# A scan's exponents from running sums: another division of work among the engines, and separate loads for attention

## What is computed

```python
a = (dt * A).reshape(bsz, nc, CHUNK, g, r).transpose(0, 3, 4, 1, 2)
a_cum = jnp.cumsum(a, axis=-1)
lmat = jnp.exp(segsum(a))                  # exp(cum[l] - cum[s]) for s <= l
cb = jnp.einsum('bclgn,bcsgn->bgcls', cc, bc)
y_diag = jnp.einsum('bgcls,bgrcls,bcsgrp->bclgrp', cb, lmat, xc)
...
y_off = jnp.einsum('bclgn,bcgrpn,bgrcl->bclgrp', cc, prev_states, jnp.exp(a_cum))
y = (y_diag + y_off).reshape(bsz, length, g, r, p)
...
y = y_f + flip(y_b) + d_skip.astype(f32).reshape(g, r)[:, :, None] * xs
gated = y.reshape(...) * jax.nn.silu(zs)
gated = gated * lax.rsqrt(jnp.mean(gated * gated, axis=-1, keepdims=True) + EPS)
```

## Time and profile before

| what | us |
|---|---|
| median of three runs (3631.65 to 3635.02) | 3632.8 |
| the profiled execution | 3636.8 |
| its span | 3635.2 |
| busy PE / DVE / ACT / POOL | 2951.8 / 2194.0 / 1100.2 / 654.5 |
| decays, first load of the carry at | 831.3 |
| scan loop: first load, last store issued | 921.0, 1389.5 |
| attention: first fill, first score | 2197.8, 2232.9 |

### The profile page before, as it was taken

The page is one execution under the profiler, slowest core; times in us unless marked ns, Lnnn a source line. Parts: engine busy times, 40 slices in busy tenths (PEclk is TensorE's granted clock), DMA queues, the critical chain, the costliest instruction groups (busy, mean ns, idle before and its releaser), DMA issues.

```text
span 3635.2 us, 33851 instructions
## 1 busy us (share of the span) xinstructions
PE 2951.8 (81%) x12604; PEld 2154.2 (59%) x12604; DVE 2194.0 (60%) x2858; ACT 1100.2 (30%) x1415; POOL 654.5 (18%) x378
## 2 busy tenths in 40 slices
PE   7999869985576666996998993879598839999993
PEld 3777746642354443444777782768344438888882
DVE  6499935326666773333563695983122269999995
ACT  3122211000011110111323411657211127777772
POOL 2322000000433330000021002545210001111111
PEclk9999979986777877998999996999798969999996
DMA  5332266413111114112544217511522539999995
GB/s 191 110 108 99 80 207 218 151 67 127 67 64 52 58 38 178 73 59 65 139 119 116 68 72 130 84 29 35 197 70 102 193 124 402 412 415 412 414 412 213
DMA packets 250064, 560.85 MB, mean 154 GB/s; under 512 B 26729, under 2 KB 157401, under 8 KB 232614
## 3 DMA queue, kind: packets, MB, share of 16 engines
q1 hardware_dynamic: 176518, 423.64, 32.5%
q0 software_dynamic: 30032, 64.18, 6.5%
q10 hardware_dynamic: 43344, 70.79, 5.2%
HBM read 438.09 MB, written 120.45 MB: 154 GB/s over the span
## 4 chain that ended last, share of the span: by engine, by line


## 5 line engine op out<-in xcount | busy, mean ns | idle before, releaser
L2327 DVE TENSOR_TENSOR e_low<-e_raw,e_high 128x4096 fp32r<-128x4096 f32 x99 | 438.0, 4426 | 69.5 <-ACT e_high L2321 69.3
L2321 ACT ACTIVATE e_high<-e_raw 128x4096 fp32r<-128x4096 f32 x99 | 359.5, 3633 | 32.8 <-DVE live L2278 26.5
L128 PE MATMUL banks<-p_w_high,p_high 128*128 128x512 f32 (+1 forms) x640 | 250.2, 391 | 18.0 <-DVE p_w_low L1455 18.0
L128 PE MATMUL banks<-p_w_low,p_high 128*128 128x512 f32 (+1 forms) x640 | 246.1, 385 | 0.0
L128 PE MATMUL banks<-p_w_high,p_low 128*128 128x512 f32 (+1 forms) x640 | 245.8, 384 | 0.0
L965 PE MATMUL banks<-s_R,mats 128*128 128x384 f32 x256 | 131.9, 678 | 130.4 <-DVE s_R L953 82.6
L128 PE MATMUL banks<-c_w,c_mT 128*128 128x512 f32 x512 | 225.8, 597 | 9.4 <-DMA c_w<-in_w_out 9.4
L128 PE MATMUL banks<-e_high,e_xhigh 128*128 128x512 f32 x528 | 211.0, 400 | 9.1 <-issue 7.3
L483 DVE SCALAR_TENSOR_TENSOR acc<-img,taps,acc 128x1024 f32<-128x1024 f32 x160 | 209.8, 1311 | 5.7
L128 PE MATMUL banks<-h_high,w_high 128*128 128x512 f32 (+1 forms) x544 | 201.2, 370 | 9.2 <-POOL w_low L355 4.5
L128 PE MATMUL banks<-e_high,e_xlow 128*128 128x512 f32 x528 | 207.9, 394 | 0.0
(11 more groups left out here) (451 smaller groups left out, 6467.9 us busy)
## 6 DMA issues: line engine op xcount, KB each, us to landing
e_raw<-in_exp_w SPq DMA_DIRECT2D x99, 2048.0 KB, 10.7
mod_w<-in_ada_w SPq DMA_DIRECT2D x24, 1024.0 KB, 6.2
s_X<-xtok SPq DMA_DIRECT2D x19, 1024.0 KB, 4.9
p_raw<-in_w_in SPq DMA_DIRECT2D x18, 1024.0 KB, 5.9
y<-e_y ACTq DMA_DIRECT2D x33, 512.0 KB, 10.5
xbcT<-res ACTq DMA_DIRECT2D x20, 640.0 KB, 2.9
xtok<-xt ACTq DMA_DIRECT2D x20, 640.0 KB, 3.7
w_raw<-in_w_in SPq DMA_DIRECT2D x12, 1024.0 KB, 6.7
```

The costliest lines, as they stand in the source:

```text
L128: last = pe.matmul(out, a, b, start=start and n == 0, stop=stop and n == len(pairs) - 1)
L2321: act.activation(self.high[p % HIGHS][:], self.raw[p % RAWS][:], ACT.Copy).then_inc(*self.high_done.up())
L2327: dve.tensor_tensor(self.low[p % HIGHS][:], self.raw[p % RAWS][:], self.high[p % HIGHS][:].bitcast(F32), ALU.subtract).then_inc(*self.low_ ...
```

## The change

**Decays.** `a` becomes local to the stage. 16 more matmuls of 128 columns compute the running sums transposed, [24 heads, 128 tokens] for each chunk and way; ACT copies them to SBUF, SP stores them to a scratch tensor `cumT` (8, 2, 24·128) in DRAM. Two small tables are new: `gap`, forward minus backward running sum, and `back`, minus the backward one.

**The scan.** For each group SP loads the rows of `cumT` to all 128 partitions (two buffers, `load_sums`). `differences` on DVE takes for each head min(rowF - gap, rowB); `exponents` takes Exp with the bias `back` for each head, in place. This gives the forward decay at and above the diagonal, and the backward one below. Both `weights` and both `timed` run on DVE. The state parts come first in PE's order (`from_states`), ACT scales them out of PSUM per head (`scale`, 12 copies of 64 columns), and PE adds them to the chunk's product with the unit matrix (`both`). DVE's `gather` is one addition. The state steps group by group. The gate's squares are ACT's. POOL has only `skip_and_weigh`. z has one buffer. The order is one loop over n with the next group's weights and the second next group's differences.

**Attention.** The fills no longer read `far` but the constant zero, POOL's and SP's loads don't wait for all of them; the first pair's operands are loaded at once, except the two last rows of `fkl`, which wait for that buffer's fill; then `far` and `fv`, the second pair, tiles and keys, `dv` last. The first weighing waits for `fv` alone.

```diff
+        sums, sums_copied, sums_stored = s1.sb("s_sums", [NH, NT, 2, P]), s1.sem("s_sums_copied"), s1.dma("s_sums_stored")
...
+        for c in range(NT):
+            for w, m in enumerate((C_LE, C_GE)):
+                last = pe.matmul(core.bank[0:NH, 3 + c // 2, 256 * (c % 2) + P * w:256 * (c % 2) + P * w + P], a[:, c, NH * w:NH * w + NH],
+                                 tables["mats"][:, m, :], start=True, stop=True)
...
+        dve.tensor_tensor(t["gap"][:], p[:, 0:NT, 0:NH], p[:, 0:NT, NH:2 * NH], ALU.subtract).then_inc(*vec.up())
+        dve.tensor_scalar(t["back"][:], p[:, 0:NT, NH:2 * NH], -1.0, None, ALU.mult).then_inc(*vec.up())
+        act.wait_ge(*summed.at(2))
+        act.activation(sums[:].rearrange("p c w n -> p (c w n)"), core.bank[0:NH, 3:7, :].rearrange("p b n -> p (b n)"), ACT.Copy).then_inc(*sums_copied.up())
+        sp.wait_ge(*sums_copied.at(1))
+        sp.dma_start(dram["cumT"].rearrange("c w (h n) -> h c w n", n=P), sums[:]).then_inc(*sums_stored.up())
...
+        def load_sums(n):
+            c, g = n // NBC, n % NBC
+            if n >= 2:
+                sp.wait_ge(*diffed.at(n - 1))
+            sp.dma_start(sums[n % 2][:].rearrange("p w h n -> p w (h n)"),
+                         row(dram["cumT"][c, :, HG * P * g:HG * P * g + HG * P])).then_inc(*sums_in[n % 2].up())
...
+        def load_z(c):
+            if c:
+                sp.wait_ge(*z_used.at(c))
...
+            for h in range(HG):
+                last = dve.scalar_tensor_tensor(out=E[n % 2][:, h, :], in0=sums[n % 2][:, 0, h, :], scalar=col("gap", c, HG * g + h),
+                                                in1=sums[n % 2][:, 1, h, :], op0=ALU.subtract, op1=ALU.min)
...
+            for h in range(HG):
+                last = act.activation(E[n % 2][:, h, :], E[n % 2][:, h, :], ACT.Exp, bias=col("back", c, HG * g + h))
...
+        def scale(n):
+            act.wait_ge(*off_summed.at(n + 1))
             if n:
+                act.wait_ge(*summed.at(n))
             for w in range(2):
+                for h in range(HG):
+                    at = slice(HP * h, HP * h + HP)
+                    last = act.activation(y2[w][:, at], core.bank[:, y0 + 1 + w, at], ACT.Copy, scale=col("ec", c, NH * w + HG * g + h))
+            last.then_inc(*scaled.up())
...
+        def both(n):
+            pe.wait_ge(*scaled.at(n + 1))
+            for w in range(2):
+                last = pe.matmul(core.bank[:, 2 + 3 * (n % 2), 0:384], mats[:, C_ID, :], y2[w][:], start=False, stop=w == 1)
+            last.then_inc(*summed.up())
...
+        def roots(c):
+            act.wait_ge(*z_used.at(c + 1))
+            if c:
+                act.wait_ge(*gated.at(c))
             for g in range(NBC):
+                act.activation(sq[:], yts[c % 2][:, 384 * g:384 * g + 384], ACT.Square, accum_out=ss[:, g:g + 1]).then_inc(*squared.up())
+                act.wait_ge(*squared.now())
+            act.activation(sd[:], ss[:], ACT.Sqrt, bias=tables["eps"][:, 0:1], scale=1.0 / 384).then_inc(*rooted.up())
...
+        load_chunk(0), load_sums(0), load_sums(1)
+        sp.dma_start(skip[:], row(dram["d_skip"])).then_inc(*rows_in.up())
+        sp.dma_start(nw[:], row(dram["ssd_norm_w"])).then_inc(*rows_in.up())
+        load_chunk(1), load_z(0)
...
+        tensor_pairs(0), skip_and_weigh(0), skip_and_weigh(1)
+        differences(0), exponents(0), differences(1), exponents(1), timed(0, 0), timed(1, 0), vector_pairs(0), weights(0)
+        for n in range(N + 1):
+            c, g = n // NBC, n % NBC
+            if n:
+                gather(n - 1), vector_step(n - 1)
+            if n < N:
+                from_states(n), scale(n), within_chunk(n), tensor_step(n), both(n)
+            if n + 1 < N:
+                weights(n + 1)
+            if n + 2 < N:
+                load_sums(n + 2), differences(n + 2), exponents(n + 2)
+            if g == 0 and c:
+                gate(c - 1), roots(c - 1)
+            if g == 1 and c:
+                if c + 1 < NT:
+                    load_chunk(c + 1)
+                if c < NT:
+                    load_z(c)
+            if g == 1 and c + 1 < NT:
+                tensor_pairs(c + 1)
+            if g == 2 and c:
+                norm(c - 1), store(c - 1)
+                if c + 1 < NT:
+                    skip_and_weigh(c + 1)
+            if g >= 2 and c + 1 < NT:
+                timed(g - 2, c + 1)
+            if g == 2 and c + 1 < NT:
+                vector_pairs(c + 1)
+        norm(NT - 1), store(NT - 1)
...
-        load_fox(0), load_tile(0), load_tile(1)
+        load_fox(0)
+        sp.wait_ge(*far_emptied)
+        sp.dma_start(far[:, :, SEQ - P:SEQ], dram["far"].rearrange("m p n -> p m n")).then_inc(*masks_in.up())
+        sp.dma_start(fv[:], pv[:, :, C_FV:C_FV + 512]).then_inc(*values_in[0].up())
+        load_fox(1), load_tile(0), load_tile(1)
...
-        load_fox(1)
+        for half in range(2):
+            sp.dma_start(dv[:, :, half, :], pv[:, :, C_DV:C_DV + HD]).then_inc(*values_in[1].up())
```

More of the change, by code:

```diff
@@ L805, in decays @@
         dve.wait_ge(*vec.at(4))
-        dve.scalar_tensor_tensor(out=t["a"][:], in0=t["dt"][:], scalar=-1.0, in1=over(an[:], 1, n),
+        dve.scalar_tensor_tensor(out=a[:], in0=t["dt"][:], scalar=-1.0, in1=over(an[:], 1, n),
                                  op0=ALU.mult, op1=ALU.mult).then_inc(*vec.up())
@@ L895, in state_space @@
         cbs = [s.sb(f"s_cb{b}", [P, 2, NBC, P]) for b in range(2)]
+        sums = [s.sb(f"s_sums{b}", [P, 2, HG, P]) for b in range(2)]
         xfs = [[s.sb(f"s_xf{b}{w}", [P, DS]) for w in range(2)] for b in range(2)]
-        R = [s.sb(f"s_R{w}", [P, HG, P]) for w in range(2)]
         E = [s.sb(f"s_E{b}", [P, HG, P]) for b in range(2)]
@@ L921, in sync, with load_chunk @@
+        def load_chunk(c):
             b, at = c % 2, slice(P * c, P * c + P)
@@ new lines, in exponents, with weights @@
+        def exponents(n):
+            c, g = n // NBC, n % NBC
+            act.wait_ge(*diffed.at(n + 1))
+            for h in range(HG):
+                last = act.activation(E[n % 2][:, h, :], E[n % 2][:, h, :], ACT.Exp, bias=col("back", c, HG * g + h))
+            last.then_inc(*E_done.up())
+        def weights(n):
+            c, g = n // NBC, n % NBC
+            dve.wait_ge(*E_done.at(n + 1))
+            dve.wait_ge(*cb_done.at(c + 1))
+            if n >= 2:
+                dve.wait_ge(*summed.at(n - 1))
+            for w in range(2):
+                last = dve.tensor_tensor(M[n % 2][w][:], E[n % 2][:], over(cbs[c % 2][:, w, g, :], 1, HG), ALU.mult)
+            last.then_inc(*M_done.up())
@@ L969, in exponents @@
-        def exponents(c, g):
-            n = 4 * c + g
-            act.wait_ge(*diffed.at(n + 1))
-            if n >= 2:
-                for w in range(2):
-                    act.wait_ge(*M_done[w].at(n - 1))
-            act.activation(E[g % 2][:].rearrange("p (a h) n -> p a (h n)", a=2), core.bank[:, 0:2, 0:384], ACT.Exp).then_inc(*E_done.up())
-        def weights(e, w, c, g):
-            n = 4 * c + g
-            e.wait_ge(*E_done.at(n + 1))
-            e.wait_ge(*cb_done.at(c + 1))
-            if n >= 2:
-                e.wait_ge(*summed.at(n - 1))
-            e.tensor_tensor(M[g % 2][w][:], E[g % 2][:], over(cbs[c % 2][:, w, g, :], 1, HG), ALU.mult).then_inc(*M_done[w].up())
@@ L1015, in gather @@
+        def both(n):
+            pe.wait_ge(*scaled.at(n + 1))
+            for w in range(2):
+                last = pe.matmul(core.bank[:, 2 + 3 * (n % 2), 0:384], mats[:, C_ID, :], y2[w][:], start=False, stop=w == 1)
+            last.then_inc(*summed.up())
+        def gather(n):
+            c, g, y0 = n // NBC, n % NBC, 2 + 3 * (n % 2)
             y = yts[c % 2][:, 384 * g:384 * g + 384]
             dve.wait_ge(*summed.at(n + 1))
-            if n:
-                dve.wait_ge(*gathered.at(n))
@@ new lines, in tensor_step, with vector_step @@
+        def tensor_step(n):
+            c, g = n // NBC, n % NBC
+            pe.wait_ge(*weighed.at(c + 1))
+            if n:
+                pe.wait_ge(*stepped.at(n))
+            pe.matmul(core.bank[:, 1, 0:384], Xs[c % 2][:, DS + NST * g:DS + NST * g + NST], xds[c % 2][:, 384 * g:384 * g + 384],
+                      start=True, stop=True).then_inc(*stepping.up())
+        def vector_step(n):
+            c, g = n // NBC, n % NBC
+            state = H[:, 384 * g:384 * g + 384]
+            dve.wait_ge(*stepping.at(n + 1))
+            dve.tensor_tensor(heads(state), heads(state), over(col("et", c, HG * g, HG), 2, HP), ALU.mult).then_inc(*vec.up())
+            dve.wait_ge(*vec.now())
+            dve.tensor_tensor(state, state, core.bank[:, 1, 0:384], ALU.add).then_inc(*stepped.up())
@@ L1068, in vector_gate, with norm @@
+        def norm(c):
+            yt = yts[c % 2]
             dve.wait_ge(*rooted.at(c + 1))
@@ L1112, in scalar @@
-        def scalar(c):
-            if c == 0:
-                exponents(0, 0), exponents(0, 1)
```

(11 more changed lines are left out.)

245 lines of the change are left out of this document (92 added, 153 removed).

## The result

The changed kernel takes 3460.2 us (median of 4 runs, 3459.0 to 3461.1) against 3632.2 (3629.2 to 3635.0): a ratio of 0.9523, 95% interval 0.9512 to 0.9535, faster by 172 us. The forecast was 3503: the sign held and so did most of the mechanism, the gain was 43 us larger than forecast, and the time lies at the very edge of the range's low end. The profiled execution took 3461.1 us (its span 3459.4), 175.7 less than that of before, where the sum had 130.0.

What follows compares the result with a forecast made beforehand. The prediction took a ring of waits, with no engine full, to bound the scan. From 3636.8 us, scan -120.8, decays +8.8 and attention -18 gave 3506.8, less 4.0 for the runs' median: 3503, range 3460 to 3580.

Steps and rivals of the forecast that it cites:

- 31/4 x 38 = 294.5: Scan loop: the 31 groups after the first, four to a chunk, at 38 us per chunk against 53.4 before.
- ACT's chain: Scan, from g = 0: gate, squares, root, scaled copies, then PE's adding matmuls, done at 15.7 us warm or 17.4 cold.
- the 1.6 us for the cold matmuls: Scan chunk: 1.6 us more because the adding matmuls run cold behind PE's wait.
- the lock: Scan: DVE and POOL keep each other out; POOL's two instructions cost DVE 2.8 us per chunk, ends 0 and 5.5.
- +8.8 forecast: Decays stage: 16 new matmuls at the low clock, copy, issue and store add 8.8 us; 6 if the clock rises, or 11.
- First group, tail, attention: Scan's first group 43.0 us, its tail 10.2 us; attention 18 us shorter, ends 8 and 27.
- the wait behind the roots: Scan: after g = 1 DVE idles for ACT's chain, a new wait of 3.8 to 5.5 us per chunk.
- The ring of waits: Old scan loop: R on DVE and POOL, differences on PE, Exp on ACT, weights, and again; it sets the pace.
- B: Rival, scan: PE stays at 1.2 GHz, 50.4 us per chunk, 3599; partial case 3540 to 3580; chance 0.17 for both.
- C: Rival, scan: ACT's copies cheap, weigh and skip hidden, no cold spells; 31.5 us per chunk, 3453; chance 0.13.
- D: Rival, scan: the row loads make it slower; at 30 us per load 63.2 us per chunk, 3698; chance 0.05.
- E: Rival, attention: the edit does nothing, as the same bytes must land before the first score; 3521; chance 0.07.

Runs made afterwards that it cites:

- pool_small: Changed kernel with both of POOL's instructions per chunk cut to one head, leaving out the other 23: 3408.7 us, 32.5 us per chunk.
- timed_early: Changed kernel with both time weightings of the next chunk put at g = 2: 3467.2 us, ratio 0.9541, 35.2 us per chunk.
- att_only: Kernel before the change with the attention edit alone: 3619.7 us, ratio 0.9963.
- roots_late: Changed kernel with squares and root moved behind the next group's scaled copies on ACT: 3463.4 us, ratio 0.9530, 34.1 us per chunk.
- both orders: Changed kernel with the reorderings of roots_late and timed_early together: 3463.0 us, ratio 0.9528, 34.5 us per chunk.
- the same orders without POOL's work: Changed kernel with both orders and POOL's two instructions cut from 24 heads to one: 3395.2 us, 29.8 us per chunk.

## What the prediction had right, and which step failed

The profiled execution was forecast at 3506.8 and took 3461.1. The failed step is the term "31/4 x 38 = 294.5" for the groups behind the first: it measured 252.5 (first addition 967.60, last 1220.13), 42.0 of the 45.7 us. It failed twice.

- **The 38: 29 us over 7.75 chunks.** The chunk took 34.3 (33.5 to 35.4). From the opening addition to the third, the forecast had ACT's chain with cold adding matmuls, 6.8 + 5.1 + 3.8 + 1.6 = 17.3; measured 15.4 (mean of six). The chain was well priced: gate done after 6.6, squares and root 4.3, copies 2.4, sum 1.6, together 14.9 in the chunk shown (forecast 15.7 with PE warm). What failed is the 1.6 us for the cold matmuls. In five of the six chunks they took 1.45 to 1.56 us, at a clock of 1.00 in the chunk shown, where PE had stood only 0.38 us before them; in the first, behind a stop of 3.72 us, they took 2.93 at 0.50, and there this stretch took 16.3. The stop and the low clock lie at g = 0 instead, where the forecast had no wait, and inside the time that ACT's chain takes anyway. From the third addition to the next opening one, the forecast had 10.5 + 6.8 + 2.8 + 0.6 = 20.7, measured 18.9: DVE's own work 16.6 instead of 17.3, the lock 2.0 in the chunk shown instead of 2.8, and of the 0.6 for waits it couldn't place 0.24.
- **The 31/4: 13 us.** It gave the first three groups and the last four the average price of a group. At the measured 34.3 they would be 60.0 us; they took 20.1 and 26.8. The first three have no gate, norm, roots or late weightings, the last four no weightings, masks or POOL work. The list of a chunk's work stood in the same text; it only had to be crossed out for the two ends.

The other terms:

- **Decays: 4.4.** +8.8 forecast, +4.4 measured. 8.2 us for 16 matmuls were priced at the low clock, 0.51 each; they took 3.67, 0.23 each, at a granted clock of 1.00 (full tiles of 128 columns take 0.26 each at that clock: L959 at 1071.89, 8 records in 1.05). So this was the forecast's own other end, "6 if the clock rises", and not a matter of the narrower stationary tile. Copy (1.85) and store (2.8) were right. The carry behind them took 0.5 us less than before.
- **First group, tail, attention: -1.** 43.0 forecast, 42.7 measured from the first load at 924.91 to 967.60, and inside it POOL's four instructions did stretch the first differences (12 in 13.31 us; 6 take 1.66 alone). Tail 10.2 against 10.0. Attention 18 against 17.5 at the first score and 16.3 at the end.

What held: the price of a difference (6 in 1.66, spaced 0.26 as forecast), no wait for the sums (4.2 us to landing, forecast 5), the place of ACT's chain. ACT's load was 22.7 us in the chunk against 25.6: the copies last 0.34 us (forecast 0.35) but start 0.20 apart (forecast 0.26). Exp and copies together are 24 x 0.29 + 48 x 0.20 = 16.6 us by these spacings, which is the estimate of 16.5 that the prediction set beside its own 19.9. That the forecast of the third addition stood within 2 us owes something to luck: it had one chain there, the trace has two of the same length. DVE alone would be there after 11.6 us; PE's late sum (1.70) and POOL's weighing (1.68) bring it to 14.9, as ACT's chain does. pool_small and timed_early each take a part of the one away, and the wait behind the roots comes up.

One row of before was misread. The 171.7 us in 32 waits before L965 count matmuls and weight loads together; PE's own matmuls stood 82.6 us there for DVE's R (16 waits) and 46.0 for POOL's. The ring of waits stands all the same, and no term of the sum used it.

Of the rivals, B (PE cold) fell as a whole: the clock in the loop is 0.89, and the low clock is that of the stretch at g = 0 and of the first chunk's sum. C has almost the right time, 3453, but its chunk of 31.5 us was not reached: the copies are cheaper than forecast, but POOL's work isn't hidden (without it the chunk is 1.8 us shorter), and there is a cold spell in each chunk. Its time comes near because of the ends of the loop, which it priced too high as well. D fell with the loads, E with att_only. The range of the chunk, 36 to 41, had no case in which the adding matmuls run warm, the reserve isn't needed and the lock is smaller, and no term let the ends of the loop be cheaper; both made the low end too high.

Not settled: why PE doesn't stop at g = 0 in the first of the six chunks, where the second addition comes after 6.5 us, and why roots_late shortens PE's stop at g = 0 to 0.7 us as well.

## What to carry to other kernels

Count first and last iterations by crossing out what they don't do, and where a price hangs on the granted clock, carry both of its values through the sum. When several delays stand between the same two hand-overs, price each as a chain from the last common point: a reordering that shortens one of them gains nothing while another is as long. Before giving elementwise work to GpSimd, compare its whole duration, as a stretch of VectorE's SBUF instructions, with what VectorE needs itself: here 2.4 to 2.5 us, where DVE has nothing else to do meanwhile, against 1.75. And a wait that is removed from a full engine may only uncover a lock that the idle time was hiding: both orders bought nothing, the same orders without POOL's work 4.7 us per chunk.
